# Last down piece of each expert layer in three parts, first gate piece behind four chunks, loop over expert groups turned

## The reference

```python
def expert_choice_moe(x, w_router, b_router, w_gate, w_up, w_down):
    b, s, d = x.shape
    cap = CAPACITY_FACTOR * s // N_EXPERTS          # 2 * 256 // 16 = 32
    logits = jnp.einsum('bsd,de->bse', x, w_router).astype(jnp.float32) + b_router.astype(jnp.float32)
    aff = jax.nn.softmax(logits, axis=-1)
    gate, idx = lax.top_k(aff.transpose(0, 2, 1), cap)
    bidx = jnp.arange(b)[:, None, None]
    xs = x[bidx, idx]
    hid = jax.nn.silu(jnp.einsum('becd,edf->becf', xs, w_gate)) * jnp.einsum('becd,edf->becf', xs, w_up)
    ys = jnp.einsum('becf,efd->becd', hid, w_down) * gate[..., None].astype(x.dtype)
    return jnp.zeros_like(x).at[bidx, idx].add(ys)

x = x + expert_choice_moe(rms_norm(x, norm_ffn), w_router, b_router, w_gate, w_up, w_down)
```

## Time and profile before

| what | us |
| --- | --- |
| median of 3 runs | 1973.77 (1973.21 to 1982.18) |
| the profiled execution | 1984.64 |
| its span, first to last instruction | 1982.8 |
| TensorE busy | 1776.7 (90%) |
| chain of work that ended last: TensorE / DMA / VectorE | 58% / 35% / 4% |

### The profile page before, as it was taken

One profiled execution on the slowest core, in us unless ns is written; L12 is line 12 of the kernel. 1 busy time (PEld: TensorE's weight loads), 2 busy tenths in 40 slices (PEclk: granted clock), 3 DMA queues, 4 the chain that ended last, 5 costly groups with the idle time before them and its releaser, 6 DMA issues.

```text
span 1982.8 us, 20841 instructions
## 1 busy us (share of the span) xinstructions
PE 1776.7 (90%) x8596; PEld 927.4 (47%) x8596; DVE 698.6 (35%) x1456; ACT 298.7 (15%) x805; POOL 121.3 (6%) x105
## 2 busy tenths in 40 slices
PE   6999999999999999999887887878999887787877
PEld 3466988644669984565332222212565322222212
DVE  1654466878536986274010010101174010010101
ACT  1124100011520000244000000000254000010000
POOL 0000000000012520220000000000120000000000
PEclk9989999999999999999899999999999999999999
DMA  9890788745425552745999999999845999999997
GB/s 346 324 340 1 230 302 300 290 165 202 139 85 169 201 193 100 240 170 202 369 424 427 426 429 427 427 428 415 259 170 215 367 425 427 426 429 427 427 428 324
DMA packets 167901, 599.64 MB, mean 302 GB/s; under 512 B 18832, under 2 KB 77968, under 8 KB 136848
## 3 DMA queue, kind: packets, MB, share of 16 engines
q1 hardware_dynamic: 167582, 598.03, 77.0%
q10 hardware_dynamic: 242, 0.53, 0.1%
HBM read 594.75 MB, written 3.80 MB: 302 GB/s over the span
## 4 chain that ended last, share of the span: by engine, by line
PE 58%; DMA 35%; DVE 4%; ACT 1%; issue 1%; DVEq 0%; POOL 0%; SPq 0%; ACTq 0%; POOLq 0%
DMA extra<-in_w_down 13%; DMA extra<-in_w_up 12%; DMA extra<-in_w_gate 11%; PE ps L1220 9%; PE ps L1578 8%; PE ps L1333 6%; PE ps L1286 6%; PE ps L1258 5%; PE ps L1077 4%; PE ps L929 3%; PE ps L1471 3%; PE ps L1165 3%; PE ps L1043 1%; PE ps L1007 1%; PE ps L1026 1%; PE ps L820 1%
## 5 line engine op out<-in xcount | busy, mean ns | idle before, releaser
L1578 PE MATMUL ps<-ring,wide 128*32 128x512 f32 x2224 | 454.2, 614 | 90.6 <-DMA ring<-in_w_up 40.8
L1578 PEld LDWEIGHTS ps<-ring,wide 128*32 128x32 f32 x2224 | 117.1, 113 | 408.9 <-issue 287.2
L3057 DVE TENSOR_TENSOR wide<-ps,wide 128x512 f32<-128x512 f32 x16 | 10.3, 686 | 532.8 <-PE ps L1578 532.8
L1578 PE MATMUL ps<-extra,wide 128*32 128x512 f32 x784 | 155.2, 630 | 44.9 <-DMA extra<-in_w_up 18.9
L1220 PE MATMUL ps<-hT,ring 128*128 128x256 f32 (+1 forms) x1088 | 183.8, 330 | 0.0
L1220 PEld LDWEIGHTS ps<-hT,ring 128*128 128x128 f32 x1088 | 166.6, 191 | 17.3 <-issue 2.9
L1333 PE MATMUL ps<-ring,hT 128*128 128x512 f32 (+2 forms) x320 | 127.3, 555 | 0.3 <-issue 0.3
L1578 PEld LDWEIGHTS ps<-extra,wide 128*32 128x32 f32 x784 | 38.3, 115 | 160.1 <-issue 95.8
L2268 DVE SCALAR_TENSOR_TENSOR extra<-ring,sc,extra 128x512 f32<-128x512 f32 x140 | 109.8, 784 | 5.2
L3062 DVE COPY wide<-ps 128x512 f32<-128x512 f32 x8 | 5.5, 691 | 256.9 <-PE ps L1578 256.9
L1333 PEld LDWEIGHTS ps<-ring,hT 128*128 128x128 f32 x320 | 60.3, 190 | 62.0 <-issue 53.4
(11 more groups left out here) (366 smaller groups left out, 2082.6 us busy)
## 6 DMA issues: line engine op xcount, KB each, us to landing
ring<-in_w_gate SPq DMA_DIRECT2D x24, 4096.0 KB, 32.0
ring<-in_w_down SPq DMA_DIRECT2D x24, 4096.0 KB, 32.0
ring<-in_w_up SPq DMA_DIRECT2D x20, 4096.0 KB, 31.0
ring<-in_w_mod SPq DMA_DIRECT2D x24, 2048.0 KB, 13.7
ring<-in_w_up SPq DMA_DIRECT2D x44, 1024.0 KB, 7.9
extra<-in_w_gate SPq DMA_DIRECT2D x8, 4096.0 KB, 35.4
extra<-in_w_up SPq DMA_DIRECT2D x8, 4096.0 KB, 31.2
extra<-in_w_down SPq DMA_DIRECT2D x8, 4096.0 KB, 30.8
```

The lines of the kernel that those rows point to most:

```text
L1578: last = mm(ps[bank + n][e * CAP:(e + 1) * CAP, :], lhs[:, k, e * CAP:(e + 1) * CAP], expert_at(n0, e, k, n * N), start=k == 0, stop=k == ...
```

## The change

Four edits.

1. The last down piece of a layer (`LAST_UNIT`) is loaded by three transfers in place of one: chunk 6 whole (2.1 MB), then the left half and the right half of chunk 7's columns (1.05 MB each). The last group's end (`last_tail`) works by these parts, and scatters and adds the left half of the columns while the right half is still under way. `x` is stored in four quarters, and the order of the four additions of the last group is by column half first.
2. In the first group of each layer, `select` covers chunks 0 to 3, then piece 0, then chunks 4 to 7.
3. The loop over groups is turned on TensorE: a turn is now the end of group g-1 (its last down piece and its scatter) and then the start of group g. On ScalarE and VectorE the loop has three turns and the last group is written out.
4. The identity products after the router are one, then one after each of the four rounds on VectorE, and one of 256 columns after the flip of the slots. Two more stand ahead of the last but one down piece of each group; the five ahead of the last down piece stay, but not in the last group.

```diff
@@ SyncE
                 for n in range(G_PAIRS + 2, GROUPS * G_TILES // PAIR):
                     sp.wait_ge(tile_done, g_used(L, 0, PAIR * pair_before(n) + PAIR - 1))
-                    pair(n)
-            for c in range(2):
-                sp.wait_ge(*x_ready(DEPTH, c, 1))
-                sp.dma_start(out[0, c * P:(c + 1) * P, :], x[:, c, :]).then_inc(sems["out_stored"], 16)
-            sp.wait_ge(sems["out_stored"], 32)
+                    if n < LAST_UNIT:
+                        pair(n)
+                last = pair_at(LAST_UNIT).rearrange("p (e k m) -> p k e m", e=EG, k=PAIR)
+                rows_ = pair_rows(LAST_UNIT).rearrange("p e k m -> p k e m")
+                sp.dma_start(last[:, 0, :, :], rows_[:, 0, :, :]).then_inc(sems["head_or_row_loaded"], 16)
+                sp.dma_start(last[:, 1, :, 0:N], rows_[:, 1, :, 0:N]).then_inc(sems["head_or_left_loaded"], 16)
+                sp.dma_start(last[:, 1, :, N:EFF], rows_[:, 1, :, N:EFF]).then_inc(arrived[pair_slot(LAST_UNIT)], 16)
+            for n in range(2):
+                for c in range(2):
+                    v = slice(n * N, (n + 1) * N)
+                    sp.wait_ge(*x_ready(DEPTH, c, n))
+                    sp.dma_start(out[0, c * P:(c + 1) * P, v], x[:, c, v]).then_inc(sems["out_stored"], 16)
+            sp.wait_ge(sems["out_stored"], 64)
@@ TensorE, after the router
-                for i in range(4):
-                    mm(ps[7][:, :], ident, tab[:, 0:N], start=True, stop=True)
-                pe.wait_ge(*s.at("b2_slots_ready", 1))
+                warm(7, 1)
+                for r in range(CAP // 8):
+                    pe.wait_ge(*s.at("b2_slots_ready", r + 1))
+                    warm(7, 1)
+                pe.wait_ge(*s.at("b2_slots_ready", CAP // 8 + 1))
...
                 last.then_inc(s.up("b2_slots_flipped"), 1)
+                warm(7, 1, T)
                 pe.wait_ge(*s.at("b2_ffn_normed", 2))
@@ TensorE, in experts()
-                            if q == GROUP_UNITS - 1:
-                                for i in range(5):
-                                    mm(ps[0][:, :], ident, tab[:, 0:N], start=True, stop=True)
+                        if q >= GROUP_UNITS - 2:
+                            warm(0, (2, 5)[q - GROUP_UNITS + 2])
@@ TensorE, start of a group
-                    select(range(4, 6))
+                    early = 4 if isinstance(g, int) else 6
+                    if early > 4:
+                        select(range(4, early))
                     pe.wait_ge(*s.at("g_rows_by_dve", 1 if isinstance(g, int) else 2))
-                    experts(0, xsT, 0, range(1))
-                    select(range(6, 8)).then_inc(s.up("g_rows_done"), 1)
+                    experts(s, g, 0, xsT, 0, range(1))
+                    select(range(early, 8)).then_inc(s.up("g_rows_done"), 1)
@@ TensorE, end of the last group, and the loop
+                def last_tail(sent):
...
+                    pe.wait_ge(sems["head_or_row_loaded"], 16 * (L + 2))
+                    last_row(ks[0], 0)
+                    last_row(ks[0], 1)
+                    pe.wait_ge(sems["head_or_left_loaded"], 16 * (L + 2))
+                    last_row(ks[1], 0).then_inc(tile_done, 1)
+                    pe.wait_ge(*s.at("g_result_by_act", 1))
+                    scatter(s, 0, 0)
+                    pe.wait_ge(*g_loaded(L, GROUPS - 1, G_TILES - PAIR))
+                    last_row(ks[1], 1).then_inc(tile_done, 1)
+                    scatter(s, 1, 0)
+                    pe.wait_ge(*s.at("g_result_by_dve", 1))
+                    scatter(s, 0, 1)
+                    scatter(s, 1, 1)
-                group(0)
+                sent = group_head(0)
                 with pe.Fori(1, GROUPS) as g:
-                    group(g)
+                    group_tail(g - 1, sent)
+                    sent = group_head(g)
+                last_tail(sent)
@@ VectorE, last group
+                    if isinstance(g, int):
+                        add(0, 0, 0)
                     dve.wait_ge(tile_done, g_used(L, g, G_TILES - 1))
                     cp(ysb[:, N:2 * N], ps[7][:, :]).then_inc(s.up("g_result_by_dve"), 1)
+                    if isinstance(g, int):
+                        for i in range(1, 4):
+                            add(i, i % 2, i // 2)
```

More of the change, by code:

```diff
@@ L1525, in flip_affinity, with warm @@
                         .then_inc(s.up("b2_affinity_flipped"), 1)
+                def warm(bank, n, cols_=N):
+                    for i in range(n):
+                        mm(ps[bank][:, 0:cols_], ident, tab[:, 0:cols_], start=True, stop=True)
                 flip_rows(0)
@@ L2041, in _, with group @@
                 s.end()
-                with act.Fori(0, GROUPS) as g:
+                def group(g):
                     s = Count(sems, L * GROUPS + g, COUNTS, "g_act_step")
@@ L3034, in _, with group @@
                 s.end()
-                with dve.Fori(0, GROUPS) as g:
+                def group(g):
                     s = Count(sems, L * GROUPS + g, COUNTS, "g_dve_step")
```

113 lines of the change are left out of this document (69 added, 44 removed).

## The result

| | kernel before | changed kernel |
|---|---|---|
| median, first measurement | 1973.21 us (1971.16 to 1982.18, 7 runs) | 1963.22 us (1962.20 to 1967.04, 7 runs) |
| ratio, 95% interval | | 0.9943 [0.9927, 0.9959] |
| median, measured again with the last experiments | 1973.40 us (1971.03 to 1982.39, 24 runs) | 1963.52 us (1961.22 to 1971.82, 7 runs) |
| ratio, 95% interval | | 0.9947 [0.9929, 0.9966] |
| profiled execution, its span, mean clock | 1984.64 us, 1982.8 us, 0.974 | 1963.22 us, 1961.4 us, 0.985 |

The changed kernel is faster by 0.57%, 8 to 14 us by the interval, 10 by the medians. Forecast: 1961.7 us, range 1957.5 to 1968.5.

The account below looks back on a forecast made before the run. Weight transfers were taken to bound the expert stages, so time is won only at their edges. Starts of 2.4 and 1.9 and ends of 3.7 and 4.1 sum to 12.1 us: 1973.8 to 1961.7 us, range 1957.5 to 1968.5.

Parts of the forecast that it names:

- start, layer 0: Layer 0's stage start: four fewer select products at full clock let piece 0 and the queue start 2.4 us earlier.
- start, layer 1: Layer 1's stage start: piece 0 earlier after select, less 0.6 us for reaching the slots' flip later; gain 1.9 us.
- end, layer 0: Layer 0, last landing to transposes: less work behind the landing takes 4.3 us instead of 8.2; gain 3.7 us.
- end, layer 1: Layer 1, last landing to end: shorter work (3.8 us) and a smaller last store (0.3 us); gain 4.1 us.
- rival D: Stage start: a later piece's issue limits the queue's restart, so the stage does not move; 1966.0 us, chance 0.08.
- late flip: Before select: five identity products instead of four reach the flip of the slots later, costing 0.6 us in layer 1.
- Rival A: Stage starts: clock still 1.2 GHz at select, gains only 1.1 and 0.6 us; 1964.3 us, chance 0.17.
- The 0.5 us: Stage ends: chunk 7's halves with 2 KB rows flow slower, so the last part lands 0.5 us later.
- Rival E: Last down piece: 2 KB rows move far slower than 386 GB/s, making the kernel slower; 1979.7 us, chance 0.05.
- Rival B: Stage tails: clock falls without the five identity products, 3 us lost a layer; 1967.7 us, chance 0.08.
- Rival C: After layer 0: next mixer's first weights land later than TensorE asks, giving back that end's gain; 1965.4 us, chance 0.10.
- The base: Whole run: the profiled execution's 10.9 us excess over the median is carried over unchanged, giving a base of 1973.8 us.

Follow-up runs that it names:

- b1: Kernel before with only the first group's select cut to four chunks ahead of piece 0, four behind it: 1971.91 us, ratio 0.9986.
- e8: Changed kernel with two final stores of 512 KB instead of four of 256 KB: 1965.76 us, ratio 0.9955.
- e9: Changed kernel, but TensorE waits for both halves of chunk 7 before its first product, then scatters: 1971.77 us, ratio 0.9992.
- t1: Kernel before with only the loop over groups turned: 1973.45 us, ratio 0.9990.
- e2: Changed kernel with the four identity products after the router in one row, none behind the flip: 1962.82 us, ratio 0.9954.
- e1: Changed kernel with six chunks selected ahead of piece 0 again: 1965.11 us, ratio 0.9963.
- e3: Changed kernel with the last down piece in one transfer and the old end of the last group: 1974.72 us, ratio 1.0011.
- e5: Changed kernel without the first of the five identity products ahead of the flip of the slots: 1965.85 us, ratio 0.9961.
- e4: Changed kernel with the old end, keeping the three transfers but waiting for all before the last piece: 1976.23 us, ratio 1.0006.
- e6: Changed kernel without the two identity products ahead of each group's last but one down piece: 1964.36 us, ratio 0.9950.

## Why the prediction was right, step by step

**The size.** Forecast 12.1 us in four terms. Measured in the one pair of traces, and as means over all traces that have the same code at the place (in brackets how many):

| term | forecast | this pair | means |
|---|---|---|---|
| start, layer 0 | 2.4 | 1.8 | 45.11 (2) to 43.14 (9): 2.0 |
| start, layer 1 | 1.9 | 2.5 | 45.26 (2) to 43.27 (9): 2.0 |
| end, layer 0 | 3.7 | 3.5 | 433.4 (4) to 429.1 (8): 4.3 |
| end, layer 1 | 4.1 | 4.1 | 437.0 (5) to 432.9 (7): 4.1 |

Left out of the means: four chunks without pacing and six with it, b1's late TensorE, e8's stores, e9's ends. Their sum is 12.4 us. The medians differ by 10.0 and 9.9; the intervals (6.7 to 14.4 us) hold 12.4 too. So each term came out near its forecast in the traces, while the medians gave 2 us less than the 12.1, and which term lacks in them is not shown.

Two things suggest that the traces flatter the change. The means of the old start rest on two traces (before and t1), and in all four of their starts the clock was low at `select`; where it stays up, as in e2 and b1 in one layer each, `select` of 24 instructions takes 2.9 us (e1) instead of 4.5. If that happens in a part of the old kernel's runs, its median holds less than the four starts show. And both of these traces look long: less what the falls ahead of the mark cost them (9.1 and 4.9 us) they stand at 1975.5 and 1975.4 us, 2 us above the old kernel's median. The gain of the end doesn't hang on this: e3 and e9 lose it in the medians as well.

**Start.** The queue's restart follows the issue, as I had argued against rival D: the dip in GB/s some 10 us behind the first issue is in all traces, no deeper with the change; the issue behind piece 1 moved by 0.9 and 1.6 us, counted from the mark (forecast 1.4), and no hole followed it; and A of 42.64 to 42.88 (clock full, flip in time) is reached in both layers. Where I was off is the late flip: I put 0.6 us on layer 1 and nothing on layer 0, and in this pair it was the other way round. In e5 it came to 1.6 us, and in e4 too (layer 0, A 44.36). The low stretch sits at a place that differs from execution to execution, so a term for it is a mean, not a property of the layer.

**Rival A** (clock still 1.2 GHz at `select`) did not happen with pacing: 1.00 in 20 of 20 starts over ten traces. Without pacing it fell in 6 of 8 (before, t1, e2, b1). So the pacing does what the text assumed. What it is worth by itself is little: A is 43.2 us on average with it, 43.5 without in the four starts that have four chunks. The rest of the 2.0 us is eight instructions moved, and that the four starts of the old kernel all had the low clock.

**End.** 32 instructions behind the landing became 8, and the wait for the copy lies under a scatter product. e4 against the changed kernel shows that it is this order, not the split of the load. From the right half's first product to the last addition's start it is 3.9 us (forecast 4.0; before 8.26 from the last piece's first product). Two other terms were mis-sized and cancel in layer 1. The 0.5 us stood for a later landing; the right half's products start 0.9 us later behind the first issue than the last piece's did (425.8 against 424.9; in layer 0 426.1 against 425.3), for I took TensorE to be idle when it lands, and it still is at a scatter product and reaches it as it lands or just behind. And the last store I put at 0.3 us; it was 0.6.

Rival E is out. Windows while the halves move, changed kernel, and below them one of the kernel before:

```profile
1361.50:1364.00 2.50, 1.92 (x16) 1.00 1.05 388
1364.00:1366.70 2.70, 1.67 (x10) 1.00 1.05 396
```

```profile
1360.00:1370.00 10.00, 7.12 (x48) 1.00 1.01 423
```

The rate did fall as forecast (386), which is 0.4 us on 2.10 MB by these rows, and e4 shows that it can't be told from the scatter of landings. The Trainium skill ("DMA: Bandwidth & Descriptors", section "Bandwidth") has 341 GB/s for a transfer of 1 MB, by which each layer would have lost 1.2 us (an estimate). The trace does not agree: these transfers stand in a queue back to back, and the rows above have 388 and 396 GB/s.

**Rival B** (clock falls in the tail) did not happen, as the windows over the ends of layers 0 and 1 show (1.00; 1.00 in the rows above too):

```profile
1365.00:1369.00 4.00, 3.28 (x16) 1.00 1.05 399
...
1954.00:1959.00 5.00, 4.22 (x15) 1.00 0.29 108
```

But e9 shows how near it is: one wait of 3.45 us (3.56 in layer 0), and it does. I had argued with "more than half is busy". That the short waits of the tail (at most 1.49 us) protect it is the likely reason, but only one longer wait was tried in each layer.

**Rival C**: the mixer's first product waits 0.39 us for no transfer. The cover held.

**Turned loop**: 0, as forecast; every segment of t1 is that of before within 0.2 us.

**The base.** I carried over "execution less median", 10.9 us, without asking where it was. Most of it, 9.1 us, was the low clock at 130 to 150 us. That this had nothing to do with the change made the carrying over sound, but I did not know that, so here I was lucky; a look at the clock by windows over the whole span would have shown it.

## What to carry to other kernels

Where a stage is bound by its transfers, time is won only at its edges: split the last transfer so that most products, the first copy and the first scatter are done when its last part lands, and order the work behind each part, since the split alone gives nothing. Keep-warm products are judged at the instructions that stand on the path: in e9 the low clock there cost 1.7 us a layer, in e6 it fell off the path and cost nothing. Before two traces are compared, find a mark ahead of the changed code and subtract what lies before it; and take a second trace of the same kernel, for what is left still moved by 2 us here.

## What was unexpected of the hardware

- TensorE ran at 1.2 GHz for 13 to 21 us from 130.3 us on in four of the 14 traces (before, e2, e4, e6), with no gap in its work as it fell, and not at all there in the others. It cost 6.2 us (e2, e4) and 9.1 us (before, e6). In two (e5, t1) the clock fell at 538 us for 10 us, behind 1.0 us of idle that stands there in the changed kernel's trace too, without a fall; that cost 4.9 us. Runs of one kernel differ by up to 11 us; that this is the reason in the runs without a trace is likely, not shown.
- The granted clock fell behind waits of 2.88 and 2.89 us in both layers of b1 and e6, but not behind waits of 2.88 to 2.90 us in the kernel before and in t1, in either layer.
- Three transfers issued in a row: in layer 1 the issues of the second and third parts hold SyncE for 9 us each instead of 0.37, and nothing behind them is lost. That the queue was full is the likely reason, no run shows it:

```profile
1921.32 0.37 SPq L805 DMA_DIRECT2D extra<-in_w_down  x1
1921.73 8.97 SPq L806 DMA_DIRECT2D extra<-in_w_down  x1
1930.74 9.55 SPq L807 DMA_DIRECT2D extra<-in_w_down  x1
```

- Two stores of 512 KB due within 0.9 us end 3.6 us behind the last addition, four of 256 KB, issued over 3.8 us, end 2.5 us behind it.
